# Gating begun inside the down pass, an unnormalised first feed-forward unit, and weight halves ahead of the step-size functions

## The reference

```python
u = rmsnorm(h, norm_mix_w)                        # first block: x/B/C, step sizes, gate z, conformer
z, xbc, dt_raw, conf_in = split(u @ w_in)
dt = softplus(dt_raw + dt_bias)                   # the "step-size functions", 16 heads x 272
h = h + concat(y_ssd, y_conf) @ w_out
act, gate = peer(h)                               # 8 heads pick 16 of 128 x 128 experts each
gate = softmax(top16 scores)
y = (gelu(x @ w_down[idx]) * gate) @ w_up[idx]
h = h + y
x = rmsnorm(h, norm_final_w, eps=1e-5)[:, 16:]    # end of the first block
h = concat(meta_2, x)                             # second block
h = h + 0.5 * swiglu(rms_norm(h, ln_ffn1, eps=1e-6))
```

## Time and profile before

| | us |
|---|---|
| runs | 2341.24, 2342.11, 2361.44 |
| median | 2342.11 |
| profiled execution, device time | 2359.45 |
| its span, first to last instruction | 2357.7 |
| mean granted TensorE clock | 0.974 |

### The profile page before, as it was taken

How to read it: one execution, slowest core, us unless ns; L and a number is a source line. 1 busy time by engine, 2 the same in 40 slices (tenths; PEclk the granted TensorE clock), 3 DMA queues, 4 the chain that set the end, 5 groups by cost and what they waited for, 6 DMA issues and landing times.

```text
span 2357.7 us, 43247 instructions
## 1 busy us (share of the span) xinstructions
PE 2242.9 (95%) x15592; PEld 2053.5 (87%) x15592; DVE 1600.2 (68%) x2897; ACT 1183.4 (50%) x1723; POOL 306.0 (13%) x211
## 2 busy tenths in 40 slices
PE   6988999999996899999799999999999999999999
PEld 5987899999996788888699988699999998558999
DVE  6797469999848755555687655666667766366774
ACT  4455247777776655555543443634344344444443
POOL 4686100000007300000111000010010000201000
PEclk8999999999998999999999999899999999999999
DMA  4432545556652266656645553145565564203555
GB/s 136 142 112 80 167 148 185 186 186 182 186 186 73 81 187 188 187 190 189 197 154 176 179 161 107 45 135 177 169 190 171 173 181 149 81 1 115 182 184 179
DMA packets 107970, 359.48 MB, mean 152 GB/s; under 512 B 12992, under 2 KB 21568, under 8 KB 107760
## 3 DMA queue, kind: packets, MB, share of 16 engines
q1 hardware_dynamic: 105792, 354.04, 48.3%
q10 hardware_dynamic: 2096, 4.36, 0.5%
HBM read 356.22 MB, written 6.46 MB: 154 GB/s over the span
## 4 chain that ended last, share of the span: by engine, by line
PE 85%; DVE 7%; issue 2%; ACT 2%; POOL 2%; DMA 1%; DVEq 0%; SPq 0%; ACTq 0%; POOLq 0%
PE ps L537 19%; PE ps L539 19%; PE ps L538 19%; PE ps L852 15%; PE ps L779 2%; PE ps L1093 1%; DVE hot_keys L1595 1%; PE ps L1168 1%; POOL ring_lo L430 1%; POOL slot_t L2413 1%; DVE ring_lo L430 1%; PE ps L1127 1%; PE ps L831 1%; DVE hw_hi L1231 1%; ACT w_hi L424 0%
## 5 line engine op out<-in xcount | busy, mean ns | idle before, releaser
L537 PE MATMUL ps<-hw_hi,w_hi 128*128 128x272 f32 (+1 forms) x3112 | 899.1, 289 | 35.4 <-DVE hw_lo L1232 11.4
L539 PE MATMUL ps<-hw_hi,ring_lo 128*128 128x272 f32 (+1 forms) x3112 | 893.2, 287 | 0.0
L538 PE MATMUL ps<-hw_lo,w_hi 128*128 128x272 f32 (+1 forms) x3112 | 892.8, 287 | 0.0
L424 ACT ACTIVATE w_hi<-ring 128x1024 fp32r<-128x1024 f32 x629 | 663.9, 1057 | 445.4 <-DMA ring<-in_ffn_in_dram 142.1
L430 DVE TENSOR_TENSOR ring_lo<-ring,w_hi 128x1024 fp32r<-128x1024 f32 x589 | 731.9, 1243 | 224.2 <-ACT w_hi L424 220.7
L537 PEld LDWEIGHTS ps<-hw_hi,w_hi 128*128 128x128 f32 x3112 | 593.2, 191 | 49.1 <-issue 29.5
L539 PEld LDWEIGHTS ps<-hw_hi,ring_lo 128*128 128x128 f32 x3112 | 593.4, 191 | 0.0
L538 PEld LDWEIGHTS ps<-hw_lo,w_hi 128*128 128x128 f32 x3112 | 591.4, 190 | 0.3
L852 PE MATMUL ps<-w_hi,hid_parts 128*128 128x512 f32 x1024 | 279.7, 395 | 2.3 <-DVE hid_parts L1622 2.3
L852 PEld LDWEIGHTS ps<-w_hi,hid_parts 128*128 128x128 f32 x1024 | 192.9, 188 | 47.4 <-issue 2.5
L2445 POOL TENSOR_TENSOR sq<-sq 128x272 f32<-128x272 f32 (+1 forms) x49 | 53.8, 1098 | 1203.1 <-ACT sq L2182 479.2
(11 more groups left out here) (395 smaller groups left out, 2517.0 us busy)
## 6 DMA issues: line engine op xcount, KB each, us to landing
ring<-in_ffn_in_dram SPq DMA_DIRECT2D x176, 512.0 KB, 3.5
ring<-in_down_dram SPq DMA_DIRECT2D x128, 512.0 KB, 3.4
ring<-in_up_dram SPq DMA_DIRECT2D x128, 512.0 KB, 3.5
ring<-in_ffn_out_dram SPq DMA_DIRECT2D x96, 512.0 KB, 3.5
ring<-in_a_in_dram SPq DMA_DIRECT2D x24, 512.0 KB, 3.5
ring<-in_xbc_dram SPq DMA_DIRECT2D x16, 512.0 KB, 3.5
ring<-in_conf_dram SPq DMA_DIRECT2D x16, 512.0 KB, 3.4
ring<-in_mix_out_dram SPq DMA_DIRECT2D x16, 512.0 KB, 3.4
```

Source lines behind the costliest of these rows:

```text
L424: nc.scalar.activation(w_hi[:, u % RING, :], ring[:, u % RING, :], ACT.Copy).then_inc(hi_done, 1)
L537: nc.tensor.matmul(bank_out, w_hi[:, b, w], hi(k0 + k), start=start and k == 0, stop=False)
L538: nc.tensor.matmul(bank_out, w_hi[:, b, w], lo(k0 + k), start=False, stop=False)
L539: last = nc.tensor.matmul(bank_out, ring_lo[:, b, w], hi(k0 + k), start=False, stop=stop and k == m - 1)
```

## The change

On the front, the two loads of xbc units 0 and 1 are issued before the small tables, and `w_heads` last; TensorE does the norm's sums before the bias table; VectorE makes a low part two tiles behind its scaling; ScalarE loads the root's table early, and makes `high` of units 4 and 5 before the step-size functions and of unit 6 before the Silus. In the down pass, the softmax and the turning of the slot tables happen after unit 111 (`TURN_AT` = 28 loops of four), `gate_low` is built in four parts between later `low`s, in banks 4 to 7, and ScalarE prepares the first two steps' `hot_a` before its last four units; the gating steps are straight code, and the high digits are built in four parts of 64 tokens. At the seam, the first unit of ffn1 is fed with h times both gains, without the final norm's factor; both norms' factors come from sums of the same squares (the second with weights), and the final norm is applied to h between the units of two later groups. Several lines of the diff that only renumber are left out.

```diff
@@ -227,8 +229,12 @@
+fresh = vec[:, VEC["conf_w"]:VEC["conf_w"] + 3 * KD]
+gain_1, weight_1, eps_both, table_in = fresh[:, 0:KD], fresh[:, KD:2 * KD], fresh[:, 16:17], fresh[:, 17:18]
+meta_sq = vec[:, VEC["conf_w"] + 3 * KD:VEC["conf_w"] + 3 * KD + KD * META].rearrange("p (k t) -> p k t", t=META)
@@ -459,12 +465,14 @@
-    sp.dma_start(w_heads[:, :, :].rearrange("p k c -> p (k c)"), a["w_heads"]).then_inc(con_loaded, 16)
+    for s in range(2):
+        load_unit("xbc", s, s)
-    for s in range(RING):
+    for s in range(2, RING):
+    sp.dma_start(w_heads[:, :, :].rearrange("p k c -> p (k c)"), a["w_heads"]).then_inc(rel_loaded, 16)
@@ -599,17 +603,17 @@
-    pe.wait_ge(con_loaded, 32)
-    pe.wait_ge(rel_loaded, 32)
+    pe.wait_ge(con_loaded, 16)
+    for k in range(KD // 2):
+        pe.wait_ge(sq_pair, k + 1)
+        last = nc.tensor.matmul(ps[:, 4, 0:T], C("mean_d"), sq[:, 2 * k, :], start=k == 0, stop=k == KD // 2 - 1)
+    last.then_inc(stat_ready, 1)
+    pe.wait_ge(rel_loaded, 48)
-    for k in range(KD // 2):
-        pe.wait_ge(sq_pair, k + 1)
-        last = nc.tensor.matmul(ps[:, 4, 0:T], C("mean_d"), sq[:, 2 * k, :], start=k == 0, stop=k == KD // 2 - 1)
-    last.then_inc(stat_ready, 1)
@@ -812,31 +816,26 @@
-    loop_8("down", normed(META), SEQ)
+    loop_8("down", normed(META), SEQ, last=TURN_AT)
+    pe.wait_ge(route_done, 1)
+    ...
-    def gates(n, b, first):
+    loop_8("down", normed(META), SEQ, first=TURN_AT)
+    pe.wait_ge(acc_free, OUT0["up"])
+    for n in range(SEQ // 8):
+        b = n % 2
-        if not first:
+        if n >= 2:
-            last = nc.tensor.matmul(ps[:, 4 + 2 * b + i // 4, (i % 4) * P:(i % 4 + 1) * P], hot_b[:, b, i, :],
+            last = nc.tensor.matmul(ps[:, 2 * b + i // 4, (i % 4) * P:(i % 4 + 1) * P], hot_b[:, b, i, :],
-    gates(0, 0, True)
-    gates(1, 1, True)
-    with pe.Fori(1, SEQ // 16) as it:
-        gates(it * 2, 0, False)
-        gates(it * 2 + 1, 1, False)
@@ -870,8 +869,36 @@
-    pe.wait_ge(h_ready, 2)
-    stats("final", META)
+    def ffn1_first(u0, bank_out, hi, lo):
+        n = 8 * NORM["ffn1"]
+        def final_sums(k):
+            if k == 0:
+                pe.wait_ge(h_ready, 4)
+            pe.wait_ge(sq_ready, n + k + 1)
+            nc.tensor.matmul(ps[:, 5, 0:SEQ], C("mean_d"), sq[:, k, META:T], start=k == 0, stop=k == KD - 1)
+            return nc.tensor.matmul(ps[:, 4, META:T], weight_1[:, k:k + 1].broadcast_to([P, P]), sq[:, k, META:T],
+                                    start=k == 0, stop=k == KD - 1)
+        pe.wait_ge(h_ready, 2)
+        for k in range(KD):
+            nc.tensor.matmul(ps[:, 4, 0:META], C("mean_d"), meta_sq[:, k, :], start=k == 0, stop=k == KD - 1)
+        pe.wait_ge(split_done, u0 + 1)
+        for k in range(KD):
+            pe.wait_ge(hw_ready, n + k + 1)
+            w = slice(k * P, (k + 1) * P)
+            nc.tensor.matmul(bank_out, w_hi[:, 0, w], hi(k), start=k == 0, stop=False)
+            nc.tensor.matmul(bank_out, w_hi[:, 0, w], lo(k), start=False, stop=False)
+            last = nc.tensor.matmul(bank_out, ring_lo[:, 0, w], hi(k), start=False, stop=k == KD - 1)
+            if k == KD - 1:
+                last.then_inc(unit_done, 1)
+            if k >= 4:
+                final_sums(k - 4)
+        for k in range(4, KD):
+            last = final_sums(k)
+        last.then_inc(stat_ready, 1)
@@ -1291,9 +1318,11 @@
+    V_.tensor_tensor(hw_full[:, 0, :], hw_full[:, 0, :], rstd[:, :], ALU.mult).then_inc(hw_scaled, 1)
+    V_.tensor_tensor(hw_full[:, 1, :], hw_full[:, 1, :], rstd[:, :], ALU.mult).then_inc(hw_scaled, 1)
-        V_.tensor_tensor(hw_full[:, k, :], hw_full[:, k, :], rstd[:, :], ALU.mult).then_inc(hw_scaled, 1)
-    for k in range(KD):
+        if k + 2 < KD:
+            V_.tensor_tensor(hw_full[:, k + 2, :], hw_full[:, k + 2, :], rstd[:, :], ALU.mult).then_inc(hw_scaled, 1)
@@ -1556,65 +1585,76 @@
...
+    while ahead[0] < RING * TURN_AT - 2:
+        low("down", ahead[0])
+        ahead[0] += 1
+    dve.wait_ge(gate_exp, 1)
+    ...
+    V_.tensor_tensor(g3, g3, bc(sums, 2, TOPK), ALU.mult).then_inc(route_done, 1)
+    for s in range(4):
+        low("down", RING * TURN_AT - 2 + s)
+    dve.wait_ge(route_turned, 1)
+    low_keys = std[:, 0:SEQ]
+    V_.tensor_copy(flat[:, 512:768], ps[:, 5, 0:256])
+    V_.tensor_copy(low_keys, ps[:, 5, 256:512]).then_inc(slots_ready, 1)
+    gate_low = ps[:, 4:8, :].rearrange("p b (t k) -> p (b t) k", k=8)
+    def low_digits(q):
+        toks = slice(64 * q, 64 * q + 64)
+        v = gate_low[:, toks, :]
+        link(V_.tensor_tensor(v, bc(low_keys[:, toks], 2, 8), bc(C("iota", 8), 1, 64), ALU.is_equal))
+        link(V_.tensor_tensor(v, v, bc(slot_t[:, 2, toks], 2, 8), ALU.mult))
+    for q in range(4):
+        low("down", RING * TURN_AT + 2 + q)
+        low_digits(q)
+    with dve.Fori(TURN_AT + 1, UNITS["down"] // RING) as it:
+        for s in range(RING):
+            low("down", s + 2, it)
+    def high_digits(q):
+        at_tok = 64 * (q % 2)
+        link(V_.tensor_tensor(high_digit[:, at_tok:at_tok + 64, :], bc(slot_t[:, 1, 64 * q:64 * q + 64], 2, 16),
+                              bc(C("iota_8", 16), 1, 64), ALU.is_equal))
+    def one_hots(n):
+        if n >= 2:
+            dve.wait_ge(gates_mm, n - 1)
+        at_tok = 8 * (n % 16)
+        V_.tensor_tensor(hot_b[:, n % 2, :, :].rearrange("p t (a k) -> p t a k", k=8),
+                         bc(high_digit[:, at_tok:at_tok + 8, :], 3, 8), bc(gate_low[:, 8 * n:8 * n + 8, :], 2, 16),
+                         ALU.mult).then_inc(hot_dve, 1)
+    def gate_hidden(n):
+        dve.wait_ge(gates_mm, n + 1)
+        v = hid[:, :, 8 * n:8 * n + 8]
+        b = n % 2
+        V_.tensor_tensor(v, v, ps[:, 2 * b:2 * b + 2, :].rearrange("p c (t i) -> p i (c t)", i=P),
+                         ALU.mult).then_inc(gated_hid, 1)
+    dve.wait_ge(unit_done, UNIT0["up"])
+    high_digits(0)
+    one_hots(0)
+    one_hots(1)
+    high_digits(1)
+    for n in range(SEQ // 8):
+        gate_hidden(n)
+        if n in (8, 16):
+            dve.wait_ge(hot_dve, n)
+            high_digits(n // 8 + 1)
+        if n + 2 < SEQ // 8:
+            one_hots(n + 2)
@@ -1628,6 +1668,18 @@
+    nf, g1 = (vec[:, VEC[n]:VEC[n] + KD] for n in ("norm_final", "ln_ffn1"))
+    dve.wait_ge(meta_loaded, 16)
+    link(V_.tensor_tensor(gain_1, nf, g1, ALU.mult))
+    link(V_.scalar_tensor_tensor(weight_1, nf, 1 / D, nf, ALU.mult, ALU.mult))
+    link(V_.tensor_scalar(weight_1, weight_1, EPS_2 / D, None, ALU.add))
+    link(V_.memset(eps_both, EPS_1 * EPS_2))
+    h_meta, scaled = h[:, :, 0:META], std[:, 0:P].rearrange("p (k t) -> p k t", t=META)
+    link(V_.tensor_tensor(scaled, h_meta, bc(g1, 2, META), ALU.mult))
+    link(V_.tensor_copy(hw_hi[:, :, 0:META], scaled))
+    link(V_.tensor_tensor(hw_lo[:, :, 0:META], scaled, hw_hi[:, :, 0:META].bitcast(F32), ALU.subtract))
+    link(V_.tensor_tensor(meta_sq, h_meta, h_meta, ALU.mult))
@@ -1636,20 +1688,32 @@
-    for j in range(KD):
+    def add_y(j):
-    invert("final", META)
-    dve.wait_ge(meta_loaded, 16)
+    def first_lo(k):
+        dve.wait_ge(hw_high, KD + k + 1)
+        V_.scalar_tensor_tensor(hw_lo[:, k, META:T], h[:, k, META:T], gain_1[:, k:k + 1], hw_hi[:, k, META:T].bitcast(F32),
+                                ALU.mult, ALU.subtract).then_inc(hw_ready, 1)
+    add_y(0)
+    add_y(1)
-        V_.scalar_tensor_tensor(h[:, j, META:T], h[:, j, META:T], V("norm_final", j), rstd[:, META:T],
+        if j + 2 < KD:
+            add_y(j + 2)
+        first_lo(j)
+    h_rstd = q_a[:, 0, 0:SEQ]
+    def final_norm(j):
+        if j == 0:
+            dve.wait_ge(h_ready, KD + 1)
+            link(V_.reciprocal(h_rstd, h_rstd))
+        V_.scalar_tensor_tensor(h[:, j, META:T], h[:, j, META:T], V("norm_final", j), h_rstd,
-    dve.wait_ge(h_ready, 16)
-    for k in range(KD):
-        gain(VEC["ln_ffn1"], k, 0)
@@ -1666,6 +1730,8 @@
+                if f == 1 and isinstance(it, int) and it:
+                    final_norm((it - 1) * RING + s)
@@ -1680,8 +1746,13 @@
-        with dve.Fori(1, FF_CHUNKS // 2) as it:
+        if f == 1:
+            group(1, False)
+            group(2, False)
+        with dve.Fori(3 if f == 1 else 1, FF_CHUNKS // 2) as it:
+        if f == 1:
+            dve.wait_ge(h_ready, 2 * KD + 1)
@@ -1955,9 +2026,10 @@
-    act.wait_ge(con_loaded, 32)
+    act.wait_ge(con_loaded, 16)
+    A_(dt_rows[:, 0, 0:1], eps[EPS_1], ACT.Sqrt)
@@ -1977,6 +2049,8 @@
+    high("xbc", 4)
+    high("xbc", 5)
@@ -1985,6 +2059,7 @@
+    high("xbc", 6)
@@ -1996,7 +2071,8 @@
-        high("xbc", e)
+        if e >= 7:
+            high("xbc", e)
@@ -2098,6 +2174,17 @@
+    def hots_act(n):
+        b = n % 2
+        rows = hot_a[:, b, :, :].rearrange("p i k -> p (i k)")
+        act.wait_ge(hot_diff, n + 1)
+        if n >= 2:
+            act.wait_ge(gates_mm, n - 1)
```

(34 more changed lines are left out.)

101 lines of the change are left out of this document (19 added, 82 removed).

## The result

| | before | after |
|---|---|---|
| runs, us | 2341.24, 2342.11, 2360.36, 2361.44 | 2315.23, 2315.35, 2318.32, 2322.22 |
| median, us | 2351.24 | 2316.84 |
| profiled execution: time, span, mean clock | 2359.45, 2357.7, 0.974 | 2315.23, 2313.4, 0.990 |

The ratio is 0.9859, with a 95% interval of 0.9831 to 0.9886: faster by 1.4%. Forecast was 2311 (2304 to 2330). The profiled executions lie 44.3 us apart and the medians 34.4; which of the two is the change's has to be found out first.

What follows compares the result with a forecast made beforehand. TensorE, busy 95% of the span, was taken as the bound, so only its idle or half-clock time could be won. 10.5 + 11.4 + 9.4 = 31.3, said as 31 us, off 2342 gave 2311 us, range 2304 to 2330.

Steps and rivals of the forecast that it cites:

- Front: Start through xbc units: earlier first unit, no wait at the fifth, no half clock behind it; 10.5 us, bounds 5 and 12.
- The fifth unit's wait and the half clock behind it: Fifth xbc unit: earlier high and low halves remove TensorE's 6.06 us wait and 2.0 us of low clock.
- The step costed at nothing: Xbc units: VectorE's step-size operations may wait behind GpSimd's low halves, convolution events queue behind; costed at nothing, bound 3 us.
- Down and gates: Down pass and gates: 10.9 from the gates' start plus 4.5 from steps less 4.0 in the pass; 11.4 us, bounds 5 and 15.
- The stall before unit 126: Down pass: ScalarE's hot_a preparations (4.4 us) against 1.5 us of slack make TensorE wait 2.9 us, bounds 1.5 and 4.2.
- The steps: Gates, first to last `gate_hidden`: 78.75 us become 74.3, saving 4.5, bounds 1 and 6.
- Seam: Up pass to ffn1: 10.0 us from an earlier start, less 0.6 for the final norm; bounds of the sum 6 and 11.
- The start of the sum: Whole kernel before: its median of the runs, put at 2342 us, from which the 31 us were taken.
- (a): Front gives gain back as step-size operations hold up events: 3 instead of 10.5 us, 2318; (a) or (b) alone 0.15.
- (b): Gates stay at their pace, ScalarE stall is 4.2: the part gives 4, 2318; (a) or (b) alone 0.15.
- (c): Routing ends late, TensorE waits for the gates after unit 111: up to 10 us, 2321; (a) with (b), or (c), 0.07.
- (d): Gates: straight code is slower; 1.0 us stall a step eats all 31, 0.8 on both engines gives 2362; chance 0.04.

Runs made afterwards that it cites:

- the fill: Kernel before, with 11 matmuls whose product nobody reads in place of TensorE's 6.06 us wait before xbc unit 4: ratio 0.9988 (0.9965 to 1.0011).
- the events first: Changed kernel, with VectorE's last six step-size operations behind convolution events 5 and 6 instead of behind event 4: ratio 0.9876 (0.9834 to 0.9918).

## Why the prediction was right, by its steps

**Front, forecast 10.5, measured 9.6** up to the end of its last unit. The first matmul and the first units are 3.0 us earlier (forecast 2.5). The fifth unit's wait and the half clock behind it are 8.3 (8.06), the half clock shown by the fill. (The working of the fifth unit's start, 35.4, has "3 x 3.0" where its result holds two units; two is right, and unit 3 ends at 35.7.) The step costed at nothing, the chain behind (VectorE's step sizes against GpSimd's low halves), is the one that came out wrong: it costs 1.7 us of its bound of 3, of which a wait of 1.1 is seen, and with the events first it costs nothing. Up to the first score the traces have 11.5 us, 1.9 more, from the clock of unchanged code between 120 and 220 us: it falls in all three kernels with the old front, and in part of those with the new one. Whether the change has a share in that is not shown.

**Down and gates, forecast 11.4, measured 13.4.** Three terms were off. The stall before unit 126 is 1.4 and not 2.9: I had charged ScalarE's whole block of 4.4 us against a slack of 1.5 us, but that slack was measured with a table load of 1.28 us in front of the high half, which is not there in the changed order. My upper bound had such a load added; it went. The delay of 2.84 us less the slack of 1.5 gives the 1.4. With the transposes, the pass is 3.1 us longer (374.8 against 371.8 from the first score), not 4.0. The start saves 16.5 - 6.1 = 10.4, forecast 10.9, because the second build waits 1.2 us for GpSimd and lies before the first product; I had put 0.8 there. The steps save 6.15 where I had 4.5: I had charged each of two builds 0.8 us of lock, but both later ones took 1.22. -3.1 + 10.4 + 6.15 = 13.45.

**Seam, forecast 9.4, measured 9.9.** Second unit 10.2 us nearer (10.0), final norm 0.3 (0.6), clock at 1.00 throughout. (The 3.47 us that the 16 sums are priced from stands in no row; the earlier trace rows have 3.62, which would make 0.3 us more.)

**The start of the sum, 2342, was 9 to 10 us too low.** It was the median of three runs; in 23 and 17 runs of the same kernel it is 2353.28 and 2351.97. With the 34.4 us of the medians, 2342 - 34.4 would have been 2308. That the forecast, 2311, is only 6 from 2316.84 is luck in part, two errors that partly cancel: 9 too low in the start (2351.24) and 3 too small in the gain (34.4).

**Rivals.** (a) happened, at 1.7 us of its 7.5. (b) no: it had the part at 4 us, and the part gives 13.4. (c) no: TensorE has no wait for the routing. (d) no: the steps are at 2.34 us on average with their builds, and putting three engines back into loops makes them no faster. The Trainium skill (Runtime: NRT & Kernel Launch, section "Instruction fetch mechanics") has a taken branch break the prefetch when its target lies outside the window of two pages; the loops' 0.05 us a turn have that sign, but they are one execution, and no view here says where the targets lie or shows an engine waiting for instructions.

The lock was the rule of the skill that mattered (SBUF — State Buffer, section "SBUF: two separate sides"): whoever starts first has the shared pair for its whole instruction. The rows agree in both directions: VectorE behind GpSimd takes 2.39 and 2.92 us for one build against 1.22, and 2.38 against 0.29 for a `TENSOR_SCALAR`; GpSimd behind VectorE takes 3.87 us for a subtraction against 1.90. The `TENSOR_SCALAR` has one tensor input alone, and the page names such a case beside that of two inputs (an operation in a 2-port mode); no view here shows the mode.

## What to carry to other kernels

A wait of TensorE can be worth more than its own length, by the half clock behind it. Not every wait has that: the one of 6.06 us had it and so had one of 1.6; those of 1.1, 1.4 and 1.8 us in the changed kernel had not (1.00 in 50 to 60, 676 to 692 and 282 to 290 us). So read the granted clock of the windows behind a wait before pricing it. Before a gain of 1% is believed, take the start from many runs, and compare stretches between anchors with unchanged stretches of the same traces as the yardstick, and end a stretch where the changed code ends. And when slack is read from a profile, look what it is made of: here it held a table load that the new order did not have. Where VectorE and GpSimd are released by the same event, look who starts first: 0.04 us decided over 1.7 us here, and an edit elsewhere turned it round.

## What the runs showed of the hardware

Over 17 runs of the kernel before, time follows the mean granted clock: 2341.88 us at 0.983, 2351.97 at 0.977, 2365.61 at 0.972, about 2.2 us for each thousandth. The changed kernel's later runs stand at 0.982 to 0.989 (medians 0.978 and about 0.985), so much of the 32 us is clock: at an equal 0.982 one run of the changed kernel took 2332.38 and three of the kernel before 2347.6 to 2347.7. That fewer and shorter waits are how the change got that clock is shown for one wait, by the fill, and seen at the places that changed; for the rest it is not shown. A fall, once it comes, is seen as 0.83 in a window of 10 us, 3.4 us at the lower level. A stretch with one fall more is 1.6 us longer, and the stretch from the last gates matmul to the transposes back steps by that: 360.7, 362.3, 364.0.
